# Grouped heads scaled and rotated inside attention in both layers; first feed-forward loads spread over four output blocks

## What is computed

```
shift, scale, gate (6 x 1024) = silu(cond) @ w_ada + b_ada        # for latents and for context
h = rms_norm(x) * norm_g * (1 + scale) + shift
z = h @ w_in                      # columns: MLA q 256, MLA kv 128, k_rope 32, grouped q 384, grouped k 128, v 128, NA 768
grouped q, k = rms_norm per head of 64, times a gain, then axial rotary (latents only)
o = attention of 4 neighbourhood heads, 6 latent (MLA) heads, 6 grouped heads
x = x + gate_a * (o @ w_out)
x = x + gate_f * swiglu(norm_ffn(x) with its own shift and scale)  # 11 blocks of 256 hidden columns
```

## Time and profile before

| what | value |
|---|---|
| median of 3 runs | 1728.08 us (1727.51 to 1728.93) |
| the profiled execution, its own time | 1726.17 us |
| its span, first to last instruction | 1724.3 us |
| granted TensorE clock, mean | 0.981 |
| PE, DVE, ACT, POOL busy | 95%, 77%, 45%, 23% of the span |

### The profile page before, as it was taken

How to read it: one execution, slowest core, us unless ns; L and a number is a source line. 1 busy time by engine, 2 the same in 40 slices (tenths; PEclk the granted TensorE clock), 3 DMA queues, 4 the chain that set the end, 5 groups by cost and what they waited for, 6 DMA issues and landing times.

```text
span 1724.3 us, 28337 instructions
## 1 busy us (share of the span) xinstructions
PE 1631.2 (95%) x10942; PEld 1562.4 (91%) x10942; DVE 1319.5 (77%) x2309; ACT 781.5 (45%) x1489; POOL 394.5 (23%) x438
## 2 busy tenths in 40 slices
PE   6999989979999999999999879999999999999997
PEld 2998878879999999999999868887999999999997
DVE  5997788857887888888879977788377767766764
ACT  3535767842633333333352356677263333333332
POOL 0033554310011211211114183333001112112111
PEclk9999999999999999999989989999999999999998
DMA  9561000064167777777537300000704665666651
GB/s 366 192 228 57 10 3 1 25 226 129 37 173 193 208 201 189 190 199 193 145 136 260 103 28 1 1 1 25 208 2 127 178 170 147 164 150 175 163 128 61
DMA packets 114138, 223.79 MB, mean 130 GB/s; under 512 B 7488, under 2 KB 39040, under 8 KB 113024
## 3 DMA queue, kind: packets, MB, share of 16 engines
q1 hardware_dynamic: 90800, 177.90, 30.1%
q0 software_dynamic: 22240, 44.14, 15.1%
q10 hardware_dynamic: 1008, 0.61, 0.1%
HBM read 218.01 MB, written 3.57 MB: 129 GB/s over the span
## 4 chain that ended last, share of the span: by engine, by line
PE 80%; DVE 11%; ACT 4%; issue 2%; DMA 2%; POOL 1%; SPq 0%; POOLq 0%; DVEq 0%; ACTq 0%
PE ps L764 24%; PE ps L765 23%; PE ps L766 23%; DVE ps L1663 4%; PE ps L1032 3%; PE ps L772 1%; PE ps L1002 1%; PE ps L849 1%; PE ps L1004 1%; PE ps L807 1%; DMA ada_wq<-in_w_adaT 1%; DVE hT L1648 1%; DMA ada_w<-in_w_adaT 1%; DVE negmax L1909 1%; ACT probs L1379 1%
## 5 line engine op out<-in xcount | busy, mean ns | idle before, releaser
L764 PE MATMUL ps<-act,dhi 128*128 128x320 f32 x704 | 218.0, 310 | 0.0
L765 PE MATMUL ps<-act,dhi 128*128 128x320 f32 x704 | 217.8, 309 | 0.0
L766 PE MATMUL ps<-act,dlo 128*128 128x320 f32 x704 | 217.8, 309 | 0.0
L2033 DVE SCALAR_TENSOR_TENSOR x<-ps,mod,x 128x512 f32<-128x512 f32 x352 | 170.5, 544 | 44.1 <-PE ps L766 44.1
L1648 DVE TENSOR_TENSOR wlo<-wraw,whi 128x1024 fp32r<-128x1024 f32 (+3 forms) x166 | 195.0, 1185 | 4.6 <-POOL wraw L2303 4.5
L766 PE MATMUL ps<-hS,wlo 128*128 128x320 f32 x640 | 198.0, 309 | 0.0
L765 PE MATMUL ps<-hS,whi 128*128 128x320 f32 x640 | 198.0, 309 | 0.0
L764 PE MATMUL ps<-hS,whi 128*128 128x320 f32 x640 | 198.0, 309 | 0.0
L764 PE MATMUL ps<-hT,whi 128*128 128x320 f32 x608 | 188.3, 310 | 2.1 <-DVE hT L1648 2.1
L766 PE MATMUL ps<-hT,wlo 128*128 128x320 f32 x608 | 188.1, 309 | 0.0
L765 PE MATMUL ps<-hT,whi 128*128 128x320 f32 x608 | 188.1, 309 | 0.0
(11 more groups left out here) (263 smaller groups left out, 4340.8 us busy)
## 6 DMA issues: line engine op xcount, KB each, us to landing
ada_w<-in_w_adaT SPq DMA_DIRECT2D x69, 512.0 KB, 5.8
draw<-in_w_down SPq DMA_DIRECT2D x22, 1024.0 KB, 6.3
wraw<-in_up_q SPq DMA_DIRECT2D x22, 768.0 KB, 6.7
wraw<-in_gate_q SPq DMA_DIRECT2D x20, 768.0 KB, 4.5
wraw<-in_gate_q POOLq DMA_DIRECT2D x20, 768.0 KB, 7.3
wraw<-in_up_q POOLq DMA_DIRECT2D x20, 768.0 KB, 7.3
wi_raw<-in_w_in SPq DMA_DIRECT2D x12, 1216.0 KB, 7.0
wraw<-in_gate_q SPq DMA_DIRECT2D x20, 512.0 KB, 3.5
```

The source lines that it names most:

```text
L764: pe.matmul(dst, lh, rh, start=start, stop=False, skip_group_check=True)
L765: pe.matmul(dst, lh, rl, start=False, stop=False, skip_group_check=True)
L766: return pe.matmul(dst, ll, rh, start=False, stop=stop, skip_group_check=True)
L2033: i = ve.scalar_tensor_tensor(out=x[:, o, c0:c1], in0=y[:, 512 - HALF + c0:512 - HALF + c1], scalar=mod[:, l, 5 * KD + o, q:q + 1], in1=x[ ...
```

## The change

Four edits. (1) `G1`, `G2` and `GR` of layer 1 run at their places in `SCHED`, as in layer 0: the ten products and the three tiles' rotation (twelve POOL instructions) ahead of attention are gone. (2) `ada_bias` and `coefs` for the second norm are made by DVE behind score unit 12 (`BIAS_AT`) in both layers, and PE's `take7` waits for the dot products themselves. (3) The gate tiles of layer 0 use four buffers: two new ones (`ada_g`, over the front of z, whose contents are used up by then) and the old two, in the order 6, 7, 0, 1. `silu_f` and gate tiles 0 and 1 are loaded ahead of `w_out` block 0, tiles 2 and 3 at block 1, tile o + 2 behind block o from block 2 on. (4) The first feed-forward loads are split over the output blocks in both layers: gate behind block 3, up behind block 4, `quarters` behind block 5, down behind block 6; the wait for the end of attention stays behind block 1.

```diff
 T_AT = {s: n for n, s in enumerate([s for s in SCHED if s[0] in ("T", "TP")])}
 S_AT = {s: n for n, s in enumerate([s for s in SCHED if s[0] == "S"])}
 NV = 5
-LATE_G = 3
+BIAS_AT = 12
 def misc_bank(what, g):
...
         s14.close()
+        s17 = ExitStack()
+        ada_g = sb("ada_g", [P, 2, DM], F32, s17)
+        s17.close()
         s2 = ExitStack()
         tn = sb("tn", [P, 2, T], F32, s2)
         hf = sb("hf", [P, 2, T], F32, s2)
...
             if l and t not in REST:
                 return 2, NEXT.index(t)
-            if t >= GATE[0]:
-                return 2, t - GATE[0]
             return (RING2, t - ADA1) if t in REST else (RING1, t - BY_PE)
         def ada_slot(l, t):
-            ring, n = ring_of(l, t)
-            slot = n % ring
-            if slot < 2:
+            slot = slot_of(l, t)
+            if l == 0 and t >= GATE[0] and slot >= 6:
+                where = ada_g[:, slot - 6]
+            elif slot < 2:
                 where = ada_w[:, slot]
             elif slot < RING2:
                 where = ada_wq[:, slot - 2]
...
                 where = ada_w1[:, slot - RING2]
             return where, ada_in[slot], 16 * (len(slot_users(l, t)) + 1), dot_at(l, t)
+        def slot_of(l, t):
+
+            if l == 0 and t >= GATE[0]:
+                return (6, 7, 0, 1)[(t - GATE[0]) % 4]
+            ring, n = ring_of(l, t)
+            return n % ring
+
         def dot_at(l, t):
             return l * len(ORDER[0]) + ORDER[l].index(t)
         def slot_users(l, t):
-            slot = ring_of(l, t)[1] % ring_of(l, t)[0]
             tiles = [(m, u) for m in range(l + 1) for u in ORDER[m]][:dot_at(l, t)]
-            return [(m, u) for m, u in tiles if ring_of(m, u)[1] % ring_of(m, u)[0] == slot]
+            return [(m, u) for m, u in tiles if slot_of(m, u) == slot_of(l, t)]
         def pT_at(n, q, c0, c1):
...
                 sp.wait_ge(v_ready, l * NV + NV)
                 sp.wait_ge(kv_out, l * 64 + 64)
                 sp.wait_ge(norm_out, l * 32 + 32)
+                if l + 1 < DEPTH:
+                    sp.dma_start(silu_f[:], a["cond"].unsqueeze(0).broadcast_to([P, 2, DM])).then_inc(cond_in, 16)
+                    for t in GATE[:2]:
+                        ada_load(l, t)
+                gate, up = a["gate_q"][l, 0], a["up_q"][l, 0]
                 for o in range(KD):
                     if o >= 2:
                         sp.wait_ge(wo_ready, l * KD + o - 1)
                     sp.dma_start(wo_raw[:, o % 2], a["w_out"][l, :, o * P:(o + 1) * P]
                                  .rearrange("(k p) n -> p k n", p=P)).then_inc(wo_in[o % 2], 16)
                     if o == 1:
-
                         sp.wait_ge(o_ready, l * 2 * NP + 2 * NP)
-                        if l + 1 < DEPTH:
-                            sp.dma_start(silu_f[:], a["cond"].unsqueeze(0).broadcast_to([P, 2, DM])).then_inc(cond_in, 16)
-                            for t in GATE[:2]:
-                                ada_load(l, t)
+                    for t in (GATE[2:4] if o == 1 else GATE[o + 2:o + 3]) if o and l + 1 < DEPTH else []:
+                        ada_load(l, t)
                     if o == 3:
-                        gate, up = a["gate_q"][l, 0], a["up_q"][l, 0]
                         sp.dma_start(wraw[:, 7:11], gate.rearrange("q p n -> p q n")).then_inc(first_in[0], 16)
+                    elif o == 4:
                         sp.dma_start(wraw[:, 11:14], up[0:3].rearrange("q p n -> p q n")).then_inc(first_in[1], 16)
                         sp.dma_start(wraw[:, S4], up[3]).then_inc(first_in[2], 16)
+                    elif o == 5:
                         quarters(l, 0, 1, None)
+                    elif o == 6:
                         down_load(l, 0)
-                    if l == 0 and o >= 3:
-                        for t in GATE[2:4] if o == 3 else GATE[o:o + 1]:
-                            ada_load(l, t)
                 def ahead(b, third):
                     tiles = AHEAD[b] if l + 1 < DEPTH else []
                     for t in tiles[2:] if third else tiles[:2]:
...
                 pe.wait_ge(z_done, l * IC * NT + IC * NT)
-                prev7[0] = (ada_done, 2, 2)
+                prev7[0] = (dots, 0, 2 * dot_at(l, REST[-1]) + 2)
                 for what, g in MISC[:3]:
                     misc_step(l, what, g)
                 pe.wait_ge(c_norm, l * NT + NT)
...
                     ve.wait_ge(gstat, l * NT + NT)
                     ve.tensor_scalar(stat[:, :, 2:10], stat[:, :, 2:10], 1.0 / 64, EPS, ALU.mult, ALU.add).then_inc(cstat_ms, 1)
-                def g_scale(t):
-                    g_divide(t)
-                    g_gain(t)
-
                 def g_divide(t):
                     zg = z[:, t, OFF_G:G_V].rearrange("p (h d) -> p h d", h=8)
                     if t == 0:
...
                     ve.tensor_scalar(z[:, t, 0:256], z[:, t, 0:256], stat[:, t, 0:1], None, ALU.mult)
                     ve.scalar_tensor_tensor(out=z[:, t, OFF_CKV:OFF_KR], in0=z[:, t, OFF_CKV:OFF_KR],
                                             scalar=stat[:, t, 1:2], in1=kv_g[:], op0=ALU.mult, op1=ALU.mult).then_inc(c_norm, 1)
-                if l:
-                    for t in range(NT):
-                        g_scale(t)
-                ada_bias(l, ADA1, GATE[0])
-                coefs(l, 1)
                 def wo_split(o):
                     ve.wait_ge(wo_hi, l * KD + o + 1)
                     lo(wo[:, o % 2, 1], wo_raw[:, o % 2], wo[:, o % 2, 0]).then_inc(wo_ready, 1)
...
                             ve.tensor_reduce(negmax[:, u:u + 1], src, AX.XY if len(src.shape) == 3 else AX.X, ALU.max,
                                              negate=True).then_inc(max_ready, 1)
                         reciprocals(ve, l, u)
+                        if u == BIAS_AT:
+                            ada_bias(l, ADA1, GATE[0])
+                            coefs(l, 1)
                     elif s[0] in ("T", "TP"):
                         n = T_AT[s]
                         if s[0] == "TP":
...
                         for dst, src, hi in v_sources(g, 1):
                             i = lo(dst, src, hi)
                         i.then_inc(v_ready, 1)
-                    elif s[0] == "G1" and l == 0:
+                    elif s[0] == "G1":
                         g_divide(s[1])
-                    elif s[0] == "G2" and l == 0:
+                    elif s[0] == "G2":
                         g_gain(s[1])
                 for o in range(1, KD):
...
             po.wait_ge(table_in, 32)
             for l in range(DEPTH):
                 def g_turn(t, turn):
-                    return (l * OWN + (24 if l == 0 or t >= LATE_G else 12) + 3 * t, 8, 64, z[:, t, OFF_G:G_V].rearrange("p (h d) -> p h d", h=8),
+                    return (l * OWN + 24 + 3 * t, 8, 64, z[:, t, OFF_G:G_V].rearrange("p (h d) -> p h d", h=8),
                             rope[:, t, 0, 0:64], rope[:, t, 1, 0:64], turn.rearrange("p (h d) -> p h d", h=8))
-
-                def g_rotate(t, turn):
-                    po.wait_ge(g_norm, l * NT + t + 1)
-                    if t:
-                        po.wait_ge(g_roped, l * 4 + t)
-                    rotate(*g_turn(t, turn)).then_inc(g_roped, 1)
-                    po.wait_ge(g_roped, l * 4 + t + 1)
                 def value_zeros(half):
...
                 po.memset(K[:, :, 1, :].bitcast(F32), 0.0).then_inc(key_zeros, 1)
                 po.wait_ge(dots, 2 * dot_at(l, REST[-1]) + 2)
                 po.memset(still[:].bitcast(F32), 0.0).then_inc(still_set, 1)
-                if l:
-                    for t in range(LATE_G):
-                        g_rotate(t, rstd[:, 0:512])
                 po.wait_ge(z_done, l * IC * NT + IC * NT)
                 settled(po, passed_po)
                 z0 = bias_h[:, 0, ZERO_OFF[0]:ZERO_OFF[0] + P]
...
                         po.wait_ge(q_roped, l * 8 + 4 + t)
                         view = qm[:, t, :].rearrange("p (h d) -> p h d", h=6)[:, :, 64:96]
                         tmp = rstd[:, 0:192].rearrange("p (h d) -> p h d", h=6)
-                        rotate(l * OWN + 12 + (3 * LATE_G if l else 0) + 3 * t, 6, 32, view, rope[:, t, 0, 64:96], rope[:, t, 1, 64:96],
+                        rotate(l * OWN + 12 + 3 * t, 6, 32, view, rope[:, t, 0, 64:96], rope[:, t, 1, 64:96],
                                tmp).then_inc(q_roped, 1)
                     elif s[0] == "S":
                         for u in in_flight(S_AT[s], 2):
...
                     elif s[0] == "QU" and s[1] == 9:
                         po.wait_ge(qm_ps, l * 2 * NT + 2 * NT)
                         value_zeros(1)
-                    elif s[0] == "GR" and s[1] >= (0 if l == 0 else LATE_G):
+                    elif s[0] == "GR":
                         _, t, j = s
                         if j == 0:
                             po.wait_ge(g_norm, l * NT + t + 1)
```

## The result

The changed kernel takes 1702.51 us (median of 4 runs, 1701.98 to 1702.98) against 1728.01 for the kernel before on the same chip (4 runs, 1727.51 to 1728.93). The ratio is 0.9855, its 95% interval 0.9839 to 0.9871: faster by 25.5 us. The prediction said 25.8 and 1702.3. The profiled execution of the changed kernel took 1701.98 us, 24.2 less than the one before.

A forecast was written before the change was run, and what follows sets the result against it. PE, busy for 95% of the span, was taken as the bound, so only its waits or lower clock mattered. Terms -14.88 - 11.31 + 0.4 = -25.8 us off the 1728.08 median gave 1702.3 us; own range 1700 to 1704, eight-in-ten 1699.5 to 1708.5.

The forecast's parts named there:

- Edit 1, 14.88 us: Layer 1's attention start: PE no longer waits for DVE's products and ada_bias, reaching block 0's split 14.88 us earlier.
- the engines get in each other's way: Rival for layer 1's attention: moved DVE and POOL work lands on the path, giving back 12.4 us, 1714.7; chance 0.04.
- Edit 2, +0.2 for each layer: Attention: ada_bias and coefs behind score unit 12 cost 0.2 us per layer, 0.4 in all.
- The bound of 2.5 us: Attention: upper cost per layer of the moved ada_bias and coefs if POOL slows both to 1.26 us.
- Edit 3, 11.31 us: Layer 0's output projection: without late loads, the eighth block is done 11.31 us earlier.
- the steps of 7.04 us: Layer 0's output projection: eight residuals come 7.04 us apart, as in layer 1.
- the estimate of 9.4 us for each load: Layer 0's output projection: each w_out block lands 9.4 us after issue; blocks 3 to 7 in time by 0.8 to 4.1 us.
- Edit 4: Layer 1's output projection: spreading the feed-forward loads gains nothing, since no split of w_out held PE up there.
- The time behind the last block: Layer 0, eighth residual to the second norm's first product: stays at 7.29 us.
- A late load: Rival for layer 0's output projection: some w_out block lands 6 us late, half the gain there lost, 1708.0; chance 0.12.
- Block 0 is late: Rival at layer 0's attention end: w_out block 0 lands 3.8 us late, delaying everything by that, 1706.1; chance 0.07.
- The case slower than before: Rival for layer 0's output projection: SP's loads and DVE's list wait on each other, 1728.5 us or more; chance 0.02.

The follow-up runs named there:

- e5: Kernel before with only ada_bias and coefs moved behind score unit 12 in both layers; 1726.54 us, ratio 0.9999, no difference.
- e3: Kernel before with four gate-tile buffers and early loads, feed-forward loads kept in one 4.5 MB pile behind block 3; 1721.1 us, ratio 0.9973.
- e4: Kernel before with its ring of two gate-tile buffers, only the feed-forward loads spread over blocks 3 to 6; 1716.91 us, ratio 0.9944.
- e1: Changed kernel with gate-tile buffers and SP's loads as before, so only the attention edits; 1713.98 us, ratio 0.9926.
- e2: Kernel before with only the output projection edits (four gate-tile buffers, early and spread loads), attention as before; 1716.0 us, ratio 0.9935.
- e9: Changed kernel measured again unaltered; 1701.93 us, ratio 0.9858 to the kernel before.
- e6: Changed kernel with 0.9 MB more unused data loaded ahead of w_out block 0 in layer 0; 1702.01 us, ratio 0.9856 to the kernel before.
- e8: Changed kernel with DVE's sums first and half of the feed-forward gate weights' split put behind the eighth residual; 1699.9 us, ratio 0.9847 to before.
- e10: e8's kernel, with the split in halves, measured again; 1699.44 us, ratio 0.9831 to the kernel before.
- e7: Changed kernel with the last two add_square ahead of DVE's 2.3 us split of feed-forward weights; 1701.01 us, ratio 0.9846 to before.

## Why the prediction was right, point by point

**Edit 1, 14.88 us: right.** The idle time is 13.47 - 0.15 = 13.32 us (forecast 13.33). Attention of layer 1 went from 200.17 to 198.92 us, where layer 0's 198.62 plus 0.2 was forecast. The windows of heads 4 to 6 show that the moved work costs nothing there; layer 0 and layer 1 after, beside the earlier trace rows:

```profile
226.54:254.01 27.47, 25.94 (x174) 22.96 (x173) 25.24 (x52) 17.94 (x43) 19.51 (x19) 1.00 0.01 4
...
1052.00:1079.50 27.50, 25.96 (x174) 22.99 (x173) 25.25 (x51) 17.95 (x44) 19.49 (x19) 1.00 0.01 4
```

DVE and POOL have layer 0's load in layer 1 now, and the stretch is 0.26 us longer than before (27.24). With this the rival "the engines get in each other's way" has fallen: single instructions do (e5's 0.69 and 1.75 us), the path doesn't. e5 shows beside it that the gain is edit 1's; edit 2 alone gives 1.7 us of the trace and no measurable time.

**Edit 2, +0.2 for each layer: right within 0.2.** DVE's `ada_bias` and `coefs` in layers 0 and 1:

```profile
187.00 0.19 DVE L1679 TENSOR_TENSOR mod<-mod,b_ada 128x48 f32<-128x48 f32 x1
187.22 0.23 DVE L1686 SCALAR_TENSOR_TENSOR coef<-mod,norm_g 128x16 f32<-128x16 f32 x1
...
1012.49 0.39 DVE L1679 TENSOR_TENSOR mod<-mod,b_ada 128x48 f32<-128x48 f32 x1
1012.92 0.30 DVE L1686 SCALAR_TENSOR_TENSOR coef<-mod,norm_g 128x16 f32<-128x16 f32 x1
```

Attention of layer 0 is 0.01 us longer than before (198.63), that of layer 1 0.29 longer than layer 0's. The bound of 2.5 us for each was far away.

**Edit 3, 11.31 us: right** (11.33), and the steps of 7.04 us too. Of the loads' estimates, each 0.65 us later by the later start, block 0 was forecast 0.9 us ahead of its need: it landed at 348.5 (issued 340.61, 7.9 us), 1.1 ahead of ACT, which didn't wait. Block 2 was there at 367.27, 2.7 earlier than estimated, block 6 at 395.63, 1.7 later, block 7 at 403.96, 1.2 later. The last has 1.1 us left to its due time: the estimate of 9.4 us for each load was fair, and its slack small. The cause was put in the right place only in part: the prediction gave the whole gain to edit 3, with the spreading inside it, and e3 and e4 show that the spreading does nine tenths of it.

**Edit 4: right in layer 1** (71.93 us from the split to the norm, 71.94 before). The prediction's "Nothing" was said of layer 1; in layer 0 it is the larger part of the gain, as just said.

**The time behind the last block, "stays" at 7.29 us: mis-sized.** It measured 8.90, 1.61 us more, which is nearly all of the 1.7 us between the forecast of 25.8 and the 24.1 of the spans. PE does the same instructions there at a clock of 0.62 where before had 0.77. PE's stand of 1.34 us ahead of it is in both kernels; how long the lower level lasts behind it differs between traces with the same code there. With the output projection of before it took 7.29, 7.31 (e1) and 8.24 us (e5), with the changed one 8.90, 8.89 (e2), 8.13 (e9) and 7.30 (e6). The two groups overlap (e3 and e4, with one of the two edits, took 5.71 and 7.31), so an effect of the change is not shown, and so few traces don't exclude one. The prediction had this term in its range, in one direction only (a better clock). That the medians came out at 25.5 all the same is partly luck, by the draw of the profiled executions: that of before was 1.8 us below its median, that of the changed kernel 0.5.

**The rivals.** A late load happens once the pile is kept (e3, 6.5 us lost). Block 0 is late with 0.9 MB more (e6), and ACT's delay of 1.57 us costs 3.2 in the trace; the prediction had priced a delay at its own length. The case slower than before was nowhere near: the longest wait of ACT for a block ended 1.1 us before it would have cost anything.

**The halves.** e8 and e10 have the lowest medians, 1699.9 and 1699.44 us. Only e10 was measured beside the changed kernel (e9): 2.5 us below it, with all five runs below e9's four, where 1.2 to 3 was expected. First residual to the norm's first product takes 54.9 us in both, against 59.3 and 58.6 in the changed kernel's two profiles. The intervals of the ratios of e9 and e10 meet at 0.9843 and 0.9844, so the medians alone don't quite settle it.

**The clock in the norm.** The twelve traces have 24 second norms. In ten, all in layer 0, PE stood 1.1 to 1.3 us at the token sums, and the granted clock was below 1.00 in nine (not in e3). In the fourteen without such a stand, layer 0 of e8 and e10 and all of layer 1, it was below 1.00 in two (layer 1 of e1 and e6, 0.76, 7.09 us). So the stand goes with the lower clock far more often than not, as e7's theory had it, but it neither always brings it nor is always needed. What decides the rest is open.

## What to carry to other kernels

If the same stage runs in another layer without the stall, its duration is the best price for removing it: both large terms came so, to 0.3 us. A wait is named by the last semaphore; ask what stands ahead of it in the list, since moving the named instruction alone may give nothing (e5). Where two edits remove the same wait, measure each alone before keeping both: spreading a pile of loads behind which a small urgent one stands gave nine tenths here, two more buffers and an early first load together one tenth. Price a short wait of PE at more than its length: in e3 and e6 a slower clock behind it added two thirds as much and more.

## What the runs showed of the hardware that was not expected

- A stretch in which PE is nearly always busy can run at the clock's lower level of 1.2 GHz for a part of it, and the part differs between traces: the norm of layer 0, each time behind PE's stand of 1.34 us, took 8.90, 8.89, 8.24, 8.13, 7.31, 7.31, 7.30, 7.29 or 5.71 us at granted clocks of 0.62, 0.62, 0.66, 0.67, 0.77, 0.77, 0.77, 0.77 and 1.00 (changed, e2, e5, e9, e1, e4, e6, before, e3). The Trainium skill, "TensorE: Matmul & The Clock Gate", section "Part 1", says that the clock goes by how busy PE has been of late. The profile's busy time does not tell these cases apart: PE was busy for 8.76 of 8.90 us at 0.62 and for 5.57 of 5.71 us at 1.00. What does was not found.
- A transfer of 512 KB on SP's queue landed 7.9 us behind its issue with 2.0 MB ahead of it, and 12.9 us behind it in e3, behind the pile of 4.5 MB.
